# A hybrid decoder layer: the projections of the first stage in two column parts instead of four groups

## The reference, cut to what matters

```
h = rmsnorm(x)
a, b, q, k, v, qm, gates = split(h @ w_in)          # 512 512 512 128 128 512 3*1024 columns
conv = silu(layernorm(depthwise_conv31(a * sigmoid(b)) + bias)) @ w_conv_out
swa  = windowed attention(q, k, v; window 128, sinks, relative bias) @ w_swa_out
mem  = attention(qm, memory of 256 rows) @ w_mem_out
x1   = x + (sum of sigmoid(gate_i) * branch_i) @ w_out
# PEER: 8 heads, 128 x 128 keys, the 16 best experts of 16384 for each head and token
eid, gate = top16(query(rmsnorm(x1)) . keys)        # 128 experts for each token
act  = gelu(sum_d xn[t, d] * w_down[eid[t, k], d])
y    = rmsnorm(x1 + sum_k gate * act * w_up[eid[t, k]])
```

## Time and profile before

| | |
|---|---|
| median of 3 runs | 3378.14 us (3375.16 to 3396.63) |
| the profiled execution | 3381.38 us, of which the span is 3379.5 us |
| PE busy in the span | 3094.5 us (92%) |
| DVE busy | 2552.1 us (76%) |
| POOL busy | 1646.9 us (49%) |
| moved by DMA | 1105.54 MB, mean 327 GB/s |

### The profile page before, as it was taken

One profiled execution on the slowest core, in us unless ns is written; L12 is line 12 of the kernel. 1 busy time (PEld: TensorE's weight loads), 2 busy tenths in 40 slices (PEclk: granted clock), 3 DMA queues, 4 the chain that ended last, 5 costly groups with the idle time before them and its releaser, 6 DMA issues.

```text
span 3379.5 us, 34200 instructions
## 1 busy us (share of the span) xinstructions
PE 3094.5 (92%) x11607; PEld 1863.5 (55%) x11607; DVE 2552.1 (76%) x5487; ACT 750.8 (22%) x2078; POOL 1646.9 (49%) x1269
## 2 busy tenths in 40 slices
PE   5988798889987899977999999999999999999898
PEld 3887686777565565444454554554554554544333
DVE  4435879888999889988798888888888875755540
ACT  2301301130113200333330420421420420420000
POOL 0001442545364567574455766865765764654420
PEclk8999899989998979989999999999999999999899
DMA  4566697969786899989999999999999999999996
GB/s 163 180 230 221 233 340 264 343 250 360 272 296 231 283 363 386 354 310 342 339 382 365 381 366 396 384 360 373 379 361 375 368 374 385 352 338 410 386 366 223
DMA packets 335472, 1105.54 MB, mean 327 GB/s; under 512 B 41315, under 2 KB 75748, under 8 KB 335147
## 3 DMA queue, kind: packets, MB, share of 16 engines
q0 software_dynamic: 172416, 625.03, 49.2%
q1 hardware_dynamic: 127598, 455.92, 36.5%
q10 hardware_dynamic: 35285, 22.43, 2.1%
HBM read 1080.81 MB, written 23.94 MB: 327 GB/s over the span
## 4 chain that ended last, share of the span: by engine, by line
PE 45%; DVE 19%; DMA 16%; issue 12%; POOL 5%; ACT 1%; SPq 0%; ACTq 0%; POOLq 0%; DVEq 0%
PE psum L1694 31%; DMA arena<-in_w_down,arena 10%; DVE arena L2052 6%; POOL arena L1366 5%; PE psum L1437 4%; PE psum L1471 3%; DMA arena<-in_w_up 3%; DVE arena L2181 2%; PE psum L1473 2%; PE psum L1487 1%; DVE arena L2076 1%; DMA arena<-in_w_q 1%; DMA arena<-in_cache_mv 1%; DMA arena<-in_w_o 0%; PE psum L1640 0%
## 5 line engine op out<-in xcount | busy, mean ns | idle before, releaser
L1366 POOL DMA_INDIRECT arena<-in_w_down,arena x1024 | 1438.7, 1405 | 972.8 <-DVE arena L2052 752.0
L1694 PE MATMUL psum<-arena 128*128 128x512 f32 x3584 | 1588.4, 596 | 38.5 <-DMA arena<-in_w_up 35.3
L2052 DVE CUSTOM_DVE_ANT_0 arena<-arena 128x1024 f32<-128x1024 f32 x1024 | 1218.0, 1221 | 233.1 <-DMA arena<-in_w_down,arena 223.6
L1694 PEld LDWEIGHTS psum<-arena 128*128 128x128 f32 x3584 | 666.2, 191 | 817.4 <-issue 739.2
L1471 PE MATMUL psum<-arena 128*128 128x256 f32 (+2 forms) x1536 | 360.7, 389 | 23.0 <-issue 23.0
L2076 DVE TENSOR_TENSOR arena<-constants,arena 128x1024 f32<-128x1024 f32 x224 | 272.9, 1222 | 108.3 <-PE psum L1437 72.1
L2525 ACT ACTIVATE arena<-arena 128x128 f32<-128x128 f32 x896 | 285.5, 390 | 305.8 <-DVE arena L2076 305.2
L1437 PEld LDWEIGHTS psum<-arena 128*128 128x128 f32 x1792 | 238.9, 196 | 159.1 <-ACT arena L2525 85.4
L1471 PEld LDWEIGHTS psum<-arena 128*128 128x128 f32 x1536 | 267.5, 194 | 101.6 <-issue 32.8
L1437 PE MATMUL psum<-arena 128*128 128x128 f32 x1792 | 245.8, 282 | 48.1 <-ACT arena L2525 39.1
L1499 PE MATMUL psum<-arena 128*128 128x256 f32 (+2 forms) x1024 | 234.4, 387 | 32.3 <-PEq L158 17.4
(11 more groups left out here) (329 smaller groups left out, 2031.8 us busy)
## 6 DMA issues: line engine op xcount, KB each, us to landing
arena<-in_w_up SPq DMA_DIRECT2D x512, 512.0 KB
arena<-in_w_gates SPq DMA_DIRECT2D x96, 768.0 KB
arena<-in_w_chunks SPq DMA_DIRECT2D x80, 512.0 KB
arena<-in_w_o SPq DMA_DIRECT2D x40, 512.0 KB
arena<-in_w_q SPq DMA_DIRECT2D x32, 512.0 KB
arena<-in_w_down,arena POOLq DMA_INDIRECT x1024, 8.1
arena<-scratch_s POOLq DMA_DIRECT2D x64, 128.0 KB
scratch_s<-arena ACTq DMA_DIRECT2D x11, 512.0 KB
```

The costliest lines, as they stand in the source:

```text
L1366: pool.indirect_dma_start(dst, None, table, bass.IndirectOffsetOnAxis(ap=idN[:, min(n, NT - 1) % 2, j:j + 1], axis=0)).then_inc(here, 16)
L1694: mm = pe.matmul(psum[:, 2 * (m % 2) + h, :], coef_block(m, s % NKEYS), wup[s % WUPR][:, h * 512:(h + 1) * 512], start=first, stop=end)
L2052: dve.tensor_tensor_reduce(row, row, rowD[slot_of["x", n]], 1.0, 0.0, ALU.mult, ALU.add, dots[:, n % 3, j:j + 1]).then_inc(row_used, 1)
```

## The change

The groups stay for `pair`, `out`, `turn`, `query` and `score`. For `ba`, `kv`, `qq`, `ls`, `lv` and the convolution there are three parts, `part_us`: block 0 (128 columns), blocks 1 to 4 (512) and blocks 5 to 7 with the samples (392). Parts 1 and 2 are worked on together: an item of part 1 is followed by its twin of part 2, which uses the same loaded chunks (`shared`), and SP reloads the buffer only after the twin (`twin`). 80 chunk loads become 44.

`uT` becomes two arrays, `uT0` for block 0 and `uTr` for the 904 others, which lies over `uT0` and over the buffer of the attention probabilities. So products of the two parts are written only after `lv` of part 0 and the third `at`; the halo goes through a small buffer `halos`; and attention beyond the first three units starts only after both `lv` of parts 1 and 2 (waits on PE in the plan, and on DVE at `as` 3).

The PE order is rewritten: `ba` of both parts for chunks 0 and 1 between the pairs of group 0; chunk 2, then 3, `kv`, `qq` and the layernorm sums of both parts around the scores of block 0; then attention units 3 to 25 woven between the pairs of groups 1 and 2, one step after each or each second pair; `out`, `turn`, `query` and `score` woven between the pairs of the next group. The sample loads move to the `out` of group 2. The convolution runs half by half, part 1 and part 2 in turn, with 2.0 us between its parts instead of 4.0. The windows of the row slots are changed.

```diff
-        UN = 3 * P + NB
-        uT = at(8256, NC, HALO + UN)
-        lnstd = at(11992, UN)
+        REST = T - P
+        uT0, uTr = at(8256, NC, HALO + P), at(8256, NC, HALO + REST)
+        lnstd = at(11992, 512)
+        halos = at(12384, NC, HALO)
...
+        part_us = [[0], [1, 2, 3, 4], [5, 6, 7, XS]]
...
+        CONV_REST = 2.0
...
+        conv_parts = [(0, i) for i in range(8)] + [(a, 4 * h + i) for h in range(2) for a in (1, 2) for i in range(4)]
...
+        def rest(i):
+            return [(kind, u) for kind, u in (("ao", i - 3), ("at", i - 2), ("as", i)) if 3 <= u < NU]
...
-        items += woven_in(pairs_of(0, 1, 2), {8: glus(1)[0:1], 12: glus(1)[1:2]})
-        for a in (1, 2, 3):
-            bs, qi, qs, st = glus(a), heads_in(a), queries(a - 1), att_steps(a)
-            old_us = group_us[a - 1]
-            items += outs(a - 1, 0) + bs[2:3] + turns(old_us[0:1]) + bs[3:4] + turns(old_us[1:2]) + qs[0:1] + [("kv", a)] + qs[1:4] + scores(old_us)
...
-            items += qi[0:2] + st[0] + qi[2:3] + st[1] + qi[3:4] + st[2] + [("ls", a)] + st[3] + [("lv", a)] + st[4] + st[5]
...
+        items += woven_in(pairs_of(0, 1, 2), {4: both("ba", 0), 10: both("ba", 1)})
+        b2 = both("ba", 2)
+        items += outs(0, 0) + b2[0:1] + turns([0]) + b2[1:2] + queries(0) + scores([0])
+        items += both("ba", 3) + both("kv") + both("qq", 0) + [("lu",)] + both("qq", 1) + both("qq", 2) + both("qq", 3)
+        items += [("ls", 1), ("ls", 2), ("lv", 1), ("lv", 2)] + rest(3) + rest(4)
+        items += rest_in(pairs_of(1, 0), range(5, 12), 1) + rest_in(pairs_of(1, 1, 2), range(12, 18), 2)
+        pr = pairs_of(2, 0)
+        qs = queries(1)
+        items += pr[0:2] + outs(1, 0) + pr[2:3] + rest(18) + pr[3:5] + turns([1]) + pr[5:6] + turns([2]) + qs[0:1] + pr[6:7] + qs[1:2]
+        items += pr[7:8] + qs[2:3] + pairs_of(2, 1, 2)[0:1] + qs[3:4] + scores([1, 2])
+        items += rest_in(pairs_of(2, 1, 2)[1:], range(19, NU + 2), 2) + rest(NU + 2)
+        pr = pairs_of(3, 0)
+        qs = queries(2)
+        items += pr[0:1] + outs(2, 0) + pr[1:2] + [("kn",), ("xs",)] + turns([3, 4]) + pr[2:3] + qs[0:1] + pr[3:4] + qs[1:2] + [("xt",)]
+        items += pr[4:5] + qs[2:3] + [("xv",)] + qs[3:4] + scores([3, 4]) + pr[5:] + pairs_of(3, 1, 2)[0:12] + [("ids0",)] + pairs_of(3, 1, 2)[12:]
...
-            elif it[0] in ("query", "ba", "qq", "kv", "mm"):
+            elif it[0] in ("query", "mm") or (it[0] in ("ba", "qq", "kv") and it[-1] < 2):
                 weights += [(k, 0), (k, 1)]
...
-        open_from = [0] * 5 + [350] * 4 + [KEPT] + [310] * 3 + [2] + [80] * 2 + [0] * 2 + [205] * 2
-        open_to = [SLOTS * (NT + 1)] * 2 + [SLOTS * (NT - 1) + 64] + [15, 15] + [SLOTS * (NT + 1)] * 5 + [370] * 3 + \
-            [390] + [370] * 2 + [50] * 2 + [350, 370]
+        open_from = [0] * 5 + [235] * 4 + [KEPT] + [185] * 3 + [2] + [128] * 2 + [0] * 2 + [205] * 2
+        open_to = [SLOTS * (NT + 1)] * 2 + [SLOTS * (NT - 1) + 64] + [30, 30] + [SLOTS * (NT + 1)] * 5 + [300] * 3 + \
+            [330] + [300] * 2 + [60] * 2 + [285, 300]
...
-                conv_due = m.now + (4.0 if convs and convs[0][0] else 0.0)
+                conv_due = m.now + (CONV_REST if convs and convs[0][0] else 0.0)
...
-                            sp.wait_ge(item_done, kp + 1)
+                            sp.wait_ge(item_done, twin(kp) + 1)
...
                     elif it[0] in ("ba", "qq"):
-                        first, n = group_cols(it[2])
+                        first, n = part_cols(it[2])
                         for j in range(2):
-                            w = load_here(k, j)
+                            w = load_here(shared(k), j)
...
                     elif it[0] == "ls":
-                        first, n = group_cols(it[1])
-                        pe.wait_ge(conv_step, NC * TAPS * (it[1] + 1))
+                        first, n = part_cols(it[1])
+                        pe.wait_ge(conv_step, taps_by[it[1]])
...
                     dve.wait_ge(item_done, k + 1)
+                    if u == 3:
+                        dve.wait_ge(item_done, item_of("lv", NP - 1) + 1)
...
                     act.wait_ge(item_done, k + 1)
                     if a:
-                        act.wait_ge(item_done, item_of("lv", a - 1) + 1)
+                        act.wait_ge(item_done, max(item_of("lv", 0), item_of("at", 2)) + 1)
```

More of the change, by code:

```diff
@@ L915, in advance @@
                             self.pe = max(self.pe, self.land(("load", load)) + cost * (len(loads) - c) / len(loads))
-                        for load in loads:
+                        held = items[k][0] in ("ba", "qq", "kv") and items[k][-1] == 2
+                        if held:
+                            loads = [load_no[w] for w in weights if w[0] == item_of(*items[k][:-1], 1)]
+                        for load in loads if twin(k) == k else []:
                             self.load_freed[load] = self.pe
@@ L951, in put @@
                 elif s[0] == "glu":
[L952 removed]
+                    self.now += 0.2 + part_cols(items[s[1]][2])[1] / 950.0
                 elif s[0] == "conv":
@@ L979, in build_kernel @@
         glus_due = list(ba_no)
-        convs = [(a, part) for a in range(NG) for part in range(8)]
+        convs = list(conv_parts)
         conv_due, halo_next, cent_next, mul_next, sconv_put = 0.0, 0, 0, 0, False
@@ L1011, in build_kernel @@
                 continue
-            if not sconv_put and m.done("glu", item_of("ba", NC - 1, NG - 1)):
+            if not sconv_put and m.done("glu", item_of("ba", NC - 1, NP - 1)):
                 m.put("sconv")
@@ L1015, in build_kernel @@
                 continue
-            if halo_next < NG - 1 and m.done("conv", halo_next, 7):
+            if halo_next < 2 and (m.done("glu", item_of("ba", NC - 1, 0)) if halo_next == 0 else
+                                  all(m.done("item", q) for q in (item_of("lv", 0), item_of("at", 2)))):
                 m.put("halo", halo_next)
```

168 lines of the change are left out of this document (90 added, 78 removed).

## The result

The changed kernel takes 3418.8 us (median, 3410.1 to 3419.8), the kernel before on the same chip 3382.5 us: a ratio of 1.0094 with an interval of 1.0060 to 1.0128 (the two medians alone give 1.0107). The profiled execution took 3417.9 us with a span of 3416.1 (3379.5 before). So the change costs 37 us by the spans, 36 by the medians, where 15 us of gain were forecast.

A forecast was written before the change was run, and what follows sets the result against it. PE and memory were both taken as full from 1565 us, PE's waits bounding the first stage. From a span of 3379.5, minus 55 for PE and plus 40 for owed rows gave 3364.5, forecast 3363 us, range 3320 to 3412.

The forecast's parts named there:

- the sum for PE behind the scores: PE between block 0's scores and the first stage's end: standing falls from 118 to 63 us.
- TensorE's gain at `ids0`: End of the first stage: PE finishes it 55 us earlier, ends 15 and 88.
- the weaving term: Attention, `out` and `query` between pairs: 45 of 68 us of waits hidden, 35 of the other 50 stay.
- PE's own work: Merged products: one of 512 columns costs the same as two of 256; saving under 1 us, taken as 0.
- The convolution: DVE taps at 0.67 us for 512 columns, saving 16 us; PE's wait at `ls` 0 to 30, taken as 5.
- The start of the gathers: Scores of block 0 and gathers start 38 us later; 0 for PE, a loss for the rows.
- The layernorm wall: PE waits for both `lv` and the 512-column silu: 10 to 40 us, taken as 20.
- The weaving and late chunks: Other PE standing: 35 us left after weaving attention between pairs, plus 3 us for late chunk loads.
- The rows owed: Gather stream: 293 rows done at `ids0` instead of 358, 65 fewer, left to the dense stage.
- Their cost: 65 rows, 34 MB, need 83 us of memory in the dense stage; 24 to 57 us lost, taken as 40.
- the waits only move: Rival: convolution and layernorm walls leave PE 0 to 15 us gain, 45 rows cost 20; 3378 to 3390; chance 0.10.
- No room: Rival: memory is full whenever PE works, so all 83 us for owed rows are paid; 3406 us; chance 0.10.

The follow-up runs named there:

- e_rest4: Changed kernel with the old 4 us pause between convolution parts instead of 2 us; ratio 1.0045 to the kernel before.
- e_wall: Changed kernel, DVE's order placing no top-k work or late rows' dots between convolution and layernorm products; ratio 1.0037 to the kernel before.
- e_two: Changed kernel with the 4 us convolution pause and the rule keeping top-k work and late rows behind the layernorm's products; ratio 0.9988 to the kernel before.
- b_win: Kernel before with only its row slot windows changed (late slots from row 255 instead of 350, middle ones 215 instead of 310); ratio 1.0104.
- a_loadtwice: Changed kernel with shared chunks loaded anew for each of parts 1 and 2 (62 loads instead of 44); ratio 1.0048 to the kernel before.
- a_taps8: Changed kernel with the convolution's accumulating taps cut to 8 columns; ratio 1.0005 to the kernel before.

## Why the prediction was wrong

3363 us was forecast, with 3412 as the upper end; it is 3418.8, and the sign is the other one. The step that failed is the sum for PE behind the scores: 63 us of standing were forecast and 106 found, so TensorE's gain at `ids0` was 13 us and not 55. Most of it is the weaving term, which took two thirds of the old waits as hidden. Step by step:

- **PE's own work: right for a product.** 32 instructions of 512 columns take 13.97 us (at 307.57), 0.437 each, and 32 of 256 columns took 7.07, half as much. The term was put at 0, and PE's busy time up to `ids0` is 1150.2 instead of 1160.2 us, 10 less, at the same mean clock of 0.93. No run says which instructions these 10 us belong to.
- **The convolution: right.** 16 taps of 512 columns took 10.69 us (at 419.26), 0.668 each; 0.67 was taken from the straight line. The wait at `ls` was 0, forecast 5.
- **The start of the gathers: 38 us forecast, 51 found.** The step counted PE's items and left out that `out` of block 0 needs DVE, which the shorter pause fills with convolution. `e_rest4` gives 13 back. The step had put the cost for PE at 0; PE stands 9 us more ahead of the scores.
- **The layernorm wall: 20 forecast, 29 found.** Its size had been worked out from the steps' own durations. The reciprocal was near (3.35 us, forecast 3.6), but with the queue clear only 4.7 us are left (`e_wall`), less than even the lower bound of 10. What was missing is what stands ahead of these steps in DVE's queue. The convolution step had this very sentence (dots that wait for rows land on PE) and applied it to `ls` alone.
- **The weaving and late chunks: 43 us of other standing forecast, 77 found** (106 - 29). This is the largest term missed. Its largest part are additions on DVE (28 us in the list of waits), 11 of them behind the top-k step that has no scores; the rest is spread over DVE's other steps and late loads. In `e_two` all standing together is 951 - 865 = 86 us, and what remains of it is again mostly waits for DVE. I had taken two thirds of the old waits as hidden without asking what DVE does in that time.
- **So TensorE's gain at `ids0`: 55 forecast, 13 found.** It stands 43 us more behind the scores than forecast and 9 more ahead of them, and is busy 10 less. Of the 42 us missing, `e_two` brings 32 back with two edits of DVE's order.
- **The rows owed: 293 forecast, 296 found.** The count came from the window and a margin, and the traces bear it out in both directions: in the changed kernel and in `b_win` the row number at which a slot is due holds the stream. What I hadn't seen is the hole from 850 to 950 us, in which no chosen experts are there to fetch.
- **Their cost: 40 forecast, 30 found in the dense stage and 50 from `ids0` to the end.** The price of a row was about right: 40 / 65 = 0.62 us forecast, 0.6 to 0.8 found at 43 to 44 rows (0.4 at 38). But only 44 of the 62 rows were still owed at the first dense product, and the stretch ahead of it, 20 us longer, was forgotten. That 40 and 50 are near each other is partly luck.

The result is thus the rival "the waits only move" for TensorE (0 to 15 us of gain) with the forecast's own rows: 3378 - 13 + 50 = 3415. I had let that rival owe 45 rows for 20 us, as if a late TensorE gave memory time. The row count hangs on the plan, not on the clock, as the prediction itself says two paragraphs earlier; priced so, the rival would have stood at 3378 - 15 + 40 to 3378 + 40, 3403 to 3418, and the upper end would have been drawn beyond it.

Two sums of the prediction don't come out as written. The rival's own terms give 3378 - 15 + 20 to 3378 + 20, 3383 to 3398, and not 3378 to 3390. And the forecast's own range joins 3378 - 88 + 57, which is 3347 and not 3335, to 3378 - 15 + 40. Its upper end pairs the smallest gain with the middle cost; with the worst cost of its own (57) it would have been 3420, just above the 3418.8 measured.

"No room" is refuted: in the dense stage a row costs a third to two thirds of its 1.27 us of memory. The limit of about 358 GB/s a core in the Trainium skill ("DMA: Bandwidth & Descriptors", Where 436 GB/s comes from) doesn't hold here either, where one core is at work: 373 GB/s over the 1837 us of the dense stage, 385 from 1200 to 1331 us.

## What to carry to other kernels

Where a planner or a hand writes a fixed order for an engine, a merged step has to be checked for what stands ahead of it in that order, above all steps that wait for a transfer: two edits of the order were worth 40 us here, as much as the merge had cost. When a stage is merged to save one engine, look for the result that starts the next stream (here the scores of blocks 1 and 2) and count how long the stream must live on what it has. Slot windows written as row numbers are part of the schedule and have to be set anew after each repair, or they take it back.

## What was unexpected of the hardware

Reading 9.4 MB once more made the first stage no slower while memory was busy 0.5 to 0.75 of the time (`a_loadtwice`, with the reserve on its order above). A tap on VectorE (DVE) has a fixed part: 0.401, 0.534 and 0.668 us at 256, 384 and 512 columns are a straight line with 0.13 us at none, and the 8 columns of `a_taps8` take 0.14 us (16 in 2.29 us). And memory gives way more than its busy share of 0.97 suggests: 22.5 MB more in the dense stage (43 rows) cost 27 to 34 us, that is 660 to 830 GB/s, some twice the mean rate. A part of them went where there was room, as in the last 136 to 140 us (322 GB/s now, 270 before).
